# The last expert block and the final norm of an MoE decoder step: loads in order, last block by halves, new order of the finals, two tiles on GpSimd

## The reference, cut to what matters

```python
h2 = rms_norm(x, norm2_g) * (1 + sc2) + sh2
y = hier_moe(h2, ...)              # top-2 of 32 experts per token: (silu(h@w1) * (h@w3)) @ w2, weighted
x = x + g2 * y                     # g2: one row of gates for the prompt, one per sample sequence
y_prompt, y_sample = rms_norm(x_prompt, final_norm_g), rms_norm(x_sample, final_norm_g)
```

## Time and profile before

| | us |
|---|---|
| median of 3 runs (1617.96 to 1618.78) | 1618.47 |
| profiled execution, its own time | 1616.88 |
| its span in the trace | 1615.1 |
| PE busy, share of the span | 1559.6 (97%) |
| DVE busy | 1259.0 (78%) |
| ACT busy | 803.2 (50%) |
| POOL busy | 365.0 (23%) |

### The profile page before, as it was taken

The page is one execution under the profiler, slowest core; times in us unless marked ns, Lnnn a source line. Parts: engine busy times, 40 slices in busy tenths (PEclk is TensorE's granted clock), DMA queues, the critical chain, the costliest instruction groups (busy, mean ns, idle before and its releaser), DMA issues.

```text
span 1615.1 us, 23296 instructions
## 1 busy us (share of the span) xinstructions
PE 1559.6 (97%) x9097; PEld 1336.2 (83%) x9097; DVE 1259.0 (78%) x1703; ACT 803.2 (50%) x874; POOL 365.0 (23%) x273
## 2 busy tenths in 40 slices
PE   5999999999999999999999998999999999999993
PEld 3777788878889999999999977888888888888771
DVE  4668887755838898887555569999999999999985
ACT  4222232334333223313243356888788788777773
POOL 2310000000000000002000202466655544543231
PEclk9999999999999999999999998999999999999997
DMA  9965223424434332234222657999999999999965
GB/s 341 318 200 181 80 86 90 139 79 148 129 91 144 118 88 77 78 88 139 78 79 87 214 198 295 374 382 387 386 369 376 381 382 377 383 384 370 370 223 230
DMA packets 219025, 361.01 MB, mean 224 GB/s; under 512 B 20166, under 2 KB 168742, under 8 KB 193562
## 3 DMA queue, kind: packets, MB, share of 16 engines
q1 hardware_dynamic: 196476, 323.10, 55.8%
q0 software_dynamic: 21792, 34.25, 7.4%
q10 hardware_dynamic: 646, 2.15, 0.3%
HBM read 363.16 MB, written 32.34 MB: 245 GB/s over the span
## 4 chain that ended last, share of the span: by engine, by line
PE 85%; DMA 6%; DVE 5%; issue 1%; DVEq 1%; ACT 1%; POOL 0%; POOLq 0%; SPq 0%; ACTq 0%
PE z L2934 16%; PE z L2936 16%; PE z L2935 16%; PE z L913 6%; PE z L915 6%; PE z L914 6%; DMA wr<-in_w_dram 3%; PE z L930 3%; PE z L932 3%; PE z L931 3%; PE q L2825 2%; PE q L904 2%; PE q L2844 1%; DVE conv L2354 1%; DMA ada_h<-in_w_ada_dram 1%
## 5 line engine op out<-in xcount | busy, mean ns | idle before, releaser
L1288 DVE TENSOR_TENSOR wl<-wr,whr 128x2048 fp32r<-128x2048 f32 x196 | 442.2, 2284 | 0.1
L1103 ACT ACTIVATE whr<-wr 128x2048 fp32r<-128x2048 f32 x196 | 372.3, 1912 | 75.0 <-DMA wr<-in_w_dram 37.8
L2934 PE MATMUL z<-h_hi,w_hi 128*128 128x272 f32 (+1 forms) x1248 | 406.7, 326 | 2.3 <-DVE h_lo L2173 1.8
L2936 PE MATMUL z<-h_hi,w_lo 128*128 128x272 f32 (+1 forms) x1248 | 402.5, 322 | 0.0
L2935 PE MATMUL z<-h_lo,w_hi 128*128 128x272 f32 (+1 forms) x1248 | 401.3, 322 | 0.0
L2173 DVE TENSOR_TENSOR w_lo<-w_raw,w_hi 128x1024 fp32r<-128x1024 f32 (+1 forms) x168 | 179.4, 1068 | 127.4 <-ACT w_hi L1872 127.4
L2934 PEld LDWEIGHTS z<-h_hi,w_hi 128*128 128x128 f32 x1248 | 234.7, 188 | 28.3 <-issue 7.4
L2936 PEld LDWEIGHTS z<-h_hi,w_lo 128*128 128x128 f32 x1248 | 234.4, 188 | 16.6
L2935 PEld LDWEIGHTS z<-h_lo,w_hi 128*128 128x128 f32 x1248 | 234.8, 188 | 15.6 <-issue 0.2
L913 PE MATMUL z<-whr,xTh 128*128 128x512 f32 x528 | 209.9, 397 | 0.4 <-DVE xTl L1288 0.4
L915 PE MATMUL z<-wl,xTh 128*128 128x512 f32 x528 | 207.1, 392 | 0.0
(11 more groups left out here) (483 smaller groups left out, 2304.6 us busy)
## 6 DMA issues: line engine op xcount, KB each, us to landing
wr<-in_w_dram SPq DMA_DIRECT2D x198, 1024.0 KB, 17.4
w_raw<-in_w_in_dram SPq DMA_DIRECT2D x104, 512.0 KB, 3.8
ada<-in_w_ada_dram SPq DMA_DIRECT2D x6, 2048.0 KB, 14.4
w_raw<-in_w_branch_dram SPq DMA_DIRECT2D x48, 256.0 KB, 2.8
w_raw<-in_w_out_dram SPq DMA_DIRECT2D x16, 512.0 KB, 4.0
ada_h<-in_w_ada_dram SPq DMA_DIRECT2D x2, 2048.0 KB, 15.1
ada_u<-in_w_ada_dram SPq DMA_DIRECT2D x2, 2048.0 KB, 9.9
ada_m<-in_w_ada_dram SPq DMA_DIRECT2D x2, 2048.0 KB, 10.8
```

What stands on the lines that cost most here:

```text
L1103: act.activation(whr[n % HN][:], wr[n % RN][:], ACT.Copy).then_inc(m_hi, 1)
L1288: return dve.tensor_tensor(out, a, b, op)
L2934: pe.matmul(out, w_hi[w][:, k, :], hi[:, k, t0:t1], start=(k == 0), stop=False)
L2936: last = pe.matmul(out, w_lo[w][:, k, :], hi[:, k, t0:t1], start=False, stop=(k == kn - 1))
```

## The change

- SP loads the last two chunks (196, 197) in their place in the order of chunks. Before, they stood behind the wait for scatter(30) and the loads of three row tiles.
- The last block's down projection runs column half by column half (j), each over all of its four k, with a count of m_c after each half; DVE multiplies, adds and ACT squares block 32's rows by halves. The mean of the second half takes the first half's sum of squares as its bias (`ehalf`).
- A new order of the finals: FINALS = 0, 1, 2, 5, samples, 6, 7, block 31's rows, block 32's rows. Tiles 3 and 4 (ASIDE) are finished by GpSimd, with tensor_scalar (times root) and tensor_tensor (times fgb), after the first half sum of block 32. SP stores 3 and 4 ahead of the samples.
- DVE: `same` moves from the end of iteration 31 into iteration 32; result of block 31 goes ahead of the roots of t0 to t2; final(1) goes ahead of gate(32). ACT: a square root is taken early, squares of t3 to t5 and their means stand ahead of gTf, and gfac of block 32 behind squares of t6 and t7.
- GpSimd: in each iteration the gather of gate rows goes behind scatter(b). The late scatters go samples first; only the first prompt one waits for all tile stores.
- The index of gate rows is worked out in three dependent steps, where it was six, with gate rows stored first in `mod_dram` (a matter of offsets); it now also reloads a prompt gate row after an empty slot. fss, fv, fr, fy, ft, eps share one tile `fin`, with the same contents.

```diff
-        FINALS = (0, 1, 2, 3, 4, 5, 6, 7, F_SMP, F_LATE[0], F_LATE[1])
-        SQUARES = (0, 1, 2, 3, 4, 5, F_LATE[0], 6, 7, F_SMP, F_LATE[1])
+        FINALS = (0, 1, 2, 5, F_SMP, 6, 7, F_LATE[0], F_LATE[1])
+        ASIDE = (3, 4)
+        SQUARES = (0, 1, 2, 3, 4, 5, 6, 7, F_LATE[0], F_SMP, F_N, F_LATE[1])
...
-            for n in range(10 * RN, NCH - 2):
+            for n in range(10 * RN, NCH):
                 load(n, CHUNKS[n][0] if CHUNKS[n][0] < NE else e_more)
...
-            tile_load(2)
-            for n in (NCH - 2, NCH - 1):
-                load(n, e_more)
-            tile_load(3)
-            for i in (7, 8):
+            for i in (5, 6, 7, 8):
                 freed(i)
                 tile_load(2 * i - 10)
                 tile_load(2 * i - 9)
...
+            for i, t in enumerate(FINALS[0:F_Y - 2]):
+                if t == F_SMP:
+                    for k, a in enumerate(ASIDE):
+                        sp.wait_ge(xg0_ok, k + 3)
+                        tile_store(a)
+                sp.wait_ge(f_y, i + 1)
...
-                if b + 1 < NB:
-                    pool.wait_ge(m_w, b + 1)
-                    gate_gather(b + 1, g2_in)
...
                 if b < NB - 2:
                     scatter(b)
+                if b + 1 < NB:
+                    pool.wait_ge(m_w, b + 1)
+                    gate_gather(b + 1, g2_in)
...
-            pool.wait_ge(f_out, 16 * F_TILE)
+            pool.wait_ge(f_sum, 2)
+            for t in ASIDE:
+                pool.tensor_scalar(yt[t][:], yt[t][:], fy[:, t:t + 1], None, ALU.mult)
+                pool.drain()
+                pool.tensor_tensor(yt[t][:], yt[t][:], fgb[:], ALU.mult).then_inc(xg0_ok, 1)
             pool.wait_ge(s_out, S_OUT + 16)
...
-                for i in range(2):
-                    for j in range(2):
-                        last = pe.matmul(z[1][:, j, :], gTf[:, 2 * c + i, :], wr[n % RN][:, i * D + j * 512:i * D + j * 512 + 512],
-                                         start=(c + i == 0), stop=(c + i == 2))
+            for j in range(2):
+                for k in range(KF):
+                    w = wr[down_no(NB - 1, k // 2) % RN]
+                    last = pe.matmul(z[1][:, j, :], gTf[:, k, :], w[:, k % 2 * D + j * 512:k % 2 * D + j * 512 + 512],
+                                     start=(k == 0), stop=(k == KF - 1))
                 last.then_inc(m_c, 1)
...
+                    if b == NB - 1:
+                        same_rows()
                     dve.wait_ge(m_c, n0 + 4)
...
+                    result((b - 1) % 2)
                     if b == NB - 1:
                         dve.wait_ge(f_par, 16)
                         roots(0, 3, 1)
-                    result((b - 1) % 2)
-                    if b == NB - 1:
-                        row_out(0, yt[0][:], P)
+                        final(0)
+                        final(1)
...
-            dve.wait_ge(m_c, NCH)
+            dve.wait_ge(m_c, NCH - 1)
             dve.wait_ge(m_w, NB)
             scattered(dve, NB - 3)
-            result((NB - 1) % 2)
-            late_sum(NB - 1)
-            final(4)
+            last = ysb[(NB - 1) % 2]
+            tt(last[:, 0:512], z[1][:, 0, :], gfac[:, 0:512], ALU.mult)
+            late_sum(NB - 1, 0, 512)
+            final(5)
+            dve.wait_ge(m_c, NCH)
+            tt(last[:, 512:D], z[1][:, 1, :], gfac[:, 512:D], ALU.mult).then_inc(m_y, 1)
+            late_sum(NB - 1, 512, D)
             roots(6, F_LATE[1], 3)
-            for n in (5, 6, 7, F_SMP, F_LATE[0]):
-                final(n)
+            final(F_SMP)
             roots(F_LATE[1], F_N, 4)
-            final(F_LATE[1])
+            for n in FINALS[5:]:
+                final(n)
```

More of the change, by code:

```diff
@@ L1173, in moe_scalar @@
                     high(9)
+            for t in (3, 4, 5):
+                tile_square(t)
+            means(3, 6, 6)
+            act.wait_ge(m_G, NB)
+            act.wait_ge(m_c, down_no(NB - 2, 1) + 1)
+            act.activation(gTf[:], q[1][:, 0, :].rearrange("p (k t) -> p k t", t=P), ACT.Copy).then_inc(m_gT, 1)
+            tile_square(6)
+            tile_square(7)
             act.wait_ge(m_y, NB - 1)
@@ L1544, in moe_vector @@
             gate()
-            late_sum(NB - 2)
-            final(1)
+            late_sum(NB - 2, 0, D)
             final(2)
-            roots(3, 6, 2)
             dve.wait_ge(*shared_pr)
```

151 lines of the change are left out of this document (69 added, 82 removed).

## The result

| | before | changed |
|---|---|---|
| median, us | 1618.22 (4 runs, 1616.57 to 1618.78) | 1628.15 (4 runs, 1626.63 to 1628.94) |
| span of the profiled execution | 1615.1 | 1626.1 |
| ratio to before | | 1.0064, 95% interval 1.0053 to 1.0076 |

The account below looks back on a forecast made before the run. TensorE and the full DMA engines set the loop's pace, so the end was summed: +1.7 - 3.2 + 1.0 + 0.45 = -0.05 on 1618.47 gave 1618.4 us. Range for 8 in 10: 1613.2 to 1622.2.

Parts of the forecast that it names:

- GpSimd's tiles: Tiles 3 and 4 on GpSimd at the end: 8 us taken, through just ahead of the stores' need; path from 9.5 us.
- The loop: Gather behind the scatter, shorter index, extra gate rows: counted at nothing, since gfac is made a full block later.
- The page's sign: Sign of gate rows making gfac late in the loop: idle time of TensorE between 1000 and 1500 us.
- The last two chunks: Chunks ahead of fgb at the end: scatter(30) lands 2.8 us later, at 1569.2, delaying the tile loads.
- rival 1: At the end, chunk loads don't delay the scatter, which lands at 1565.9: 1613.2 us; chance 0.32 with partial forms.
- The gate, the matmuls: Block 32: gate at 1581.8, gTf behind G's end at 1583.1, matmuls starting about 1 us later than before.
- a term of +1.7: End of the last matmul: 1592.1 plus 0.6 for a lowered clock after TensorE's idle time, against 1591.0 before.
- The 12.0 us for t5: Tail tile loads: t5, the sixth half-megabyte, landing about 12.0 us after the first tile issue.
- Rival 3: Clock stays low through all 16 matmuls: 7.1 us more, or 3.6 if for half; 1621.4 to 1624.9; chance 0.06.
- After the last matmul: DVE's work behind the last matmul takes 9.8 us, 3.2 less than 13.0; store order then loses 0.45.
- contention: Some eight DVE operations beside GpSimd's tiles slowed: 1.0 us in all, bounded by nothing and by 8 us.
- rival 2: GpSimd and DVE exclude each other in the tail; at 5.0 us lost by DVE, 1622.4 us; chance 0.12.

Follow-up runs that it names:

- e6: Changed kernel plus one early GpSimd drain ahead of its wait for the late sums: 1619.98 us, ratio 1.0018 to the kernel before.
- e1: Changed kernel with the gate gather back ahead of the block's scatter: 1628.06 us, ratio 1.0061 to the kernel before.
- e2: Changed kernel with the gate index of before, no gate rows reloaded after empty slots: 1626.31 us, ratio 1.0053 to the kernel before.
- e16: Changed kernel with both loop edits undone (gather first, gate index of before), GpSimd's tiles kept: 1625.23 us, ratio 1.0049 to the kernel before.
- e9: Changed kernel with gather first, gate index of before, and tiles 3 and 4 finished by DVE: 1616.50 us, ratio 1.0005 to the kernel before.
- e3: Changed kernel with tiles 3 and 4 finished by DVE, none by GpSimd: 1618.28 us, ratio 1.0006 to the kernel before.
- e10: e9 with the last two chunks loaded as before, behind the tile loads of t0 to t2: 1619.84 us, ratio 1.0020 to the kernel before.
- e15: e9 plus early GpSimd drain, block 32's gate ahead of roots, gTf ahead of squares, last two chunks loaded as before: 1613.35 us, ratio 0.9977.
- e5: Kernel before plus one GpSimd drain ahead of its wait for the stores: 1612.38 us, ratio 0.9975 to the kernel before.
- e17: Kernel before with both loop edits, gather behind the scatter and the new rule for gate rows: 1620.19 us, ratio 1.0019.
- e12: Kernel before with only the new rule reloading gate rows after empty slots: 1620.53 us, ratio 1.0017 to the kernel before.

## Why the prediction was wrong, point by point

**"GpSimd's tiles. ... Two tiles: 4.4 to 13.6 us; I take 8": this step failed, and is the main one.** It measured 19.0. The operations are 13.1 of them (3.81 + 3.01 + 3.80 + 0.16 + 2.34), inside the bounds but at their upper end, because one tensor_scalar took 2.8 to 3.8 us, above the 1.1 to 2.3 that I had scaled from a row of 512 columns. Some 2.6 of the 13.1 lie beside DVE's finals: these tensor_scalars take 2.83 and tensor_tensor 2.34 where none is in the way (e6). The other 5.9 are a cost that the sum had no term for: the drain between the operations, GpSimd's first behind its transfers (5.89 or 5.90 also in e1, e2 and e16; e6: behind an earlier drain the gap is 0.16). They started when I said, 1.8 us ahead of the end of the last matmul. The prediction's own threshold, "from 9.5 us on they would be the path", is passed by 9.5, and in the changed kernel they are the path; at 11.6 us, in e6, they are not, since DVE is held up there and ends later still. The end's drain gives 3.6 of that back, and what stands behind the last tile is longer than behind a DVE final, since SP's stores of the samples, t6 and t7 queue behind it and the samples' store needs 3.3 us and more to land. Measured as a difference of kernels: 7.1 us (e16 against e9), 9.4 (the changed kernel against e3).

**"The loop. ... Together: nothing": this step failed too.** The cover, "microseconds are left", was wrong: by going behind the scatter the gather is let go by DVE's result, not by ACT's factors, and then needs 10.9 us, so gfac is late in nearly every block of the loop (31 waits). Nor were the extra gate rows nothing: 1.5 MB (35.72 instead of 34.25 MB on GpSimd's DMA queue) in a loop in which the DMA engines are full cost 2.7 us by themselves. Each edit alone costs 4.0 or 2.7, both together 3.1 in the kernel before. The page's sign was named (idle time of TensorE between 1000 and 1500 us) and came, as a busy share of 98.6 instead of a full one. In the changed kernel this is worth nothing to 5 us.

**The last two chunks, "the dearest place": right.** Scatter(30) was issued at 1562.91, and SP's tile loads, which it releases, start at 1572.90: 10.0 us, where I took 10.1, 10.1 in e9, and 6.7 with the chunks late (e10, e15). So the two chunks cost the scatter 3.4 us; that it is one straggling DMA engine that passes this on, no row shows, since the rows have only the mean of the engines. The forecast of rival 1 falls. That this term cost nothing in the end (e15) I had not seen: the same bytes are moved either way, and with the late chunks t5 and the last matmuls wait for them.

**The gate, the matmuls.** With the loop of before (e9) the gate starts at 1581.61 (forecast 1581.8), gTf is copied at 1584.38 (forecast from about 1583.1), the last matmul ends at 1592.4, +1.4 against a term of +1.7. The 12.0 us for t5 were not what its own proportion gives (11.2); t5's square starts 13.1 us after the first tile issue in e9, and this is why gTf came later than forecast. The clock did fall, to 0.50 in 1586 to 1588 us of the changed kernel, and was on its way back by 1590; the 16 matmuls took 7.33, 0.2 over the full clock's 7.13, and the shared products ahead of them 1.91 where they had taken 1.02, so that the matmuls start 0.5 behind the end of gTf's copy and not at once: some 0.65 in all, and 0.6 was about right. Rival 3, the clock low for longer, came in part only in e10, where TensorE stood 6.1 us: 2.8 us more, not 3.6 to 7.1.

**After the last matmul, and contention.** e9's time, +0.8 (0.6 less to 2.3 more), stands against the sum of the terms without GpSimd's tiles: +1.7 - 3.2 + 1.2 + 0.45 = +0.15. Of the two finals that are back on DVE only one, 1.2, stands behind the last matmul; the other lies in DVE's idle time ahead of it. In e9's trace these terms measure +1.4, -1.9 (with the final) and +0.15, and its span is 0.4 shorter. So these terms hold, as far as the error lets one say. Contention was counted at 1.0 for some eight operations. It is not spread: beside tensor_tensor DVE stands until GpSimd is through, 2.1 us a time, once in the changed kernel and twice in e6. Beside tensor_scalar it depends on the operation: a final takes 1.28, its usual time, but the first two root steps behind the second half wait for GpSimd's end, 1597.40 against 1597.37:

```profile
1596.82 0.58 DVE L1446 TENSOR_SCALAR fin<-fin 128x4 f32<-128x4 f32 x1
```

GpSimd waits too: the tensor_scalars that start inside a DVE final take 3.8 instead of 2.8 us and end 2.7 us behind that final. So rival 2's mechanism was there in part. In the changed kernel it did not decide, since GpSimd was late by far more; in e6, where DVE needs 14.7 us from the second half's result on against a forecast of 9.8, it sets the end. The Trainium skill, "SBUF — State Buffer", section "SBUF: two separate sides", has the rule for a whole instruction; the rows of tensor_tensor agree to 0.01 us, but a DVE final in the middle of a tensor_scalar is not held (the sample tile's, 1.27 us at 1602.19 in e6).

## What to carry to other kernels

Before work goes to an idle engine, count what its first use costs there and every wait between its operations, not only the operations; and see who is queued behind the result, here three stores and four scatters. An edit that moves a small transfer behind a large one in the same queue changes what lets it go: look for the consumer's wait, and in a loop whose DMA engines are full no extra row is free. If the profile ends in a long drain, try one early, where the engine idles anyway and long enough: its own row was 14 to 17 us long here.

## What the runs showed of the hardware that I had not expected

- A drain of GpSimd that came first after its indirect DMAs cost 4 to 6 us once: 5.9 in the changed kernel between two operations, 8.3 against 4.0 us for the last drain of the kernel before and of e5. All kernels here agree: the last drain takes 7.6 to 8.3 us in the eight that have no drain of this kind ahead of it, and 3.8 to 4.0 in the ten that have one. One early drain, under an idle stretch of 31 us, took 4.1 us off a kernel whose engines were not touched otherwise. Its own row is 16.5 us long (14.4 in e6), from the last gathers' issue on, so in a place where GpSimd has work it could cost more than it saves. What GpSimd does in it is not settled by these runs. The Trainium skill, "GPSIMD Engine Reference", section 2.1, tells of about 6 us at the first call of freshly loaded code, without a row in the profile; the 5.9 us agree in size, but whether they are that, no run here shows.
- GpSimd's operations on 128 × 1,024 fp32: tensor_scalar 2.83 us, 3.8 where it starts inside a DVE final; tensor_tensor 2.34, 3.01 where it does. DVE does both in one operation of 1.28.
- Waits that would end last in different stretches did not add up: the late gather alone cost 4.0 us, the extra rows alone 2.7, both 3.1. With both (e17) ACT's waits for chunks, 71.4 us in e12, were no longer among its longest, and TensorE's share in 1400 to 1500 us was 99.3 instead of 96.1.
